# First layer's shift and scale biases as rows of a transposed parameter block, constants issued by ScalarE

## The reference, cut to what matters

```
ada = jax.nn.silu(cond) @ w_ada[l] + b_ada[l]            # w_ada[l]: 1024 x 6144, float32
sh1, sc1, g1, sh2, sc2, g2 = jnp.split(ada[:, None, :], 6, axis=-1)
u = layer_norm(x) * (1 + sc1) + sh1
m = even_mixer(u, w_in_even, ...)        # layer 0: attention and pooling; layer 1: conv and Fourier
x = layer_norm(ALPHA * x + g1 * (m @ w_out[l]), ln_g[l, 0], ln_b[l, 0])
u = layer_norm(x) * (1 + sc2) + sh2
x = layer_norm(ALPHA * x + g2 * conv_ffn(u), ln_g[l, 1], ln_b[l, 1])
```

## Time and profile before

| | before |
|---|---|
| median of 3 runs | 3036.16 us (3031.93 to 3036.25) |
| the profiled execution, its own time | 3033.15 us |
| its span | 3031.4 us |
| TensorE / VectorE / ScalarE / GpSimd busy | 91% / 52% / 31% / 14% |
| mean granted clock of TensorE | 0.959 |

### The profile page before, as it was taken

One profiled execution on the slowest core, in us unless ns is written; L12 is line 12 of the kernel. 1 busy time (PEld: TensorE's weight loads), 2 busy tenths in 40 slices (PEclk: granted clock), 3 DMA queues, 4 the chain that ended last, 5 costly groups with the idle time before them and its releaser, 6 DMA issues.

```text
span 3031.4 us, 36504 instructions
## 1 busy us (share of the span) xinstructions
PE 2768.7 (91%) x13992; PEld 2439.5 (80%) x13992; DVE 1565.9 (52%) x2166; ACT 936.5 (31%) x1417; POOL 419.2 (14%) x222
## 2 busy tenths in 40 slices
PE   5698799779999999999997899989899999999997
PEld 2387577558899999999994789968899999999996
DVE  0326688746555555555557333336555555555557
ACT  1611477635322222222225421124522222222123
POOL 0032377525000000000007000004200000000002
PEclk9799799979999999999998899989999999999999
DMA  8710100022311111111118231222311111111111
GB/s 291 258 46 6 42 1 1 7 78 77 132 42 42 42 42 42 42 42 42 38 37 288 67 91 42 69 77 77 125 42 42 42 42 42 42 42 42 42 35 77
DMA packets 172260, 202.26 MB, mean 67 GB/s; under 512 B 6843, under 2 KB 125207, under 8 KB 172179
## 3 DMA queue, kind: packets, MB, share of 16 engines
q1 hardware_dynamic: 171859, 200.83, 20.2%
q10 hardware_dynamic: 320, 0.33, 0.0%
HBM read 181.80 MB, written 19.33 MB: 66 GB/s over the span
## 4 chain that ended last, share of the span: by engine, by line
PE 69%; DVE 13%; ACT 6%; issue 5%; DMA 4%; POOL 2%; SPq 0%; ACTq 0%; DVEq 0%; POOLq 0%
PE ps L1845 37%; PE ps L2057 17%; PE ps L1823 7%; POOL p_low L749 2%; DMA late_w<-in_w_ada 2%; DVE small L1434 2%; DMA ada_w<-in_w_ada 2%; DVE dw_ctx L1269 1%; ACT ln_u L887 1%; DVE ft L1515 1%; PE ps L1977 1%; PE ps L1792 1%; DVE dctx L1537 1%; DVE uw L1269 1%; ACT p_top L812 1%
## 5 line engine op out<-in xcount | busy, mean ns | idle before, releaser
L1845 PE MATMUL ps<-act_b,uw 128*128 128x384 f32 x4608 | 819.5, 339 | 10.1 <-DVE act_b L1269 6.4
L1845 PEld LDWEIGHTS ps<-act_b,uw 128*128 128x128 f32 x4608 | 816.0, 189 | 11.9 <-DVE act_b L1269 6.9
L1845 PE MATMUL ps<-act_a,uw 128*128 128x384 f32 x3456 | 616.5, 340 | 5.5 <-DVE act_a L1269 5.5
L1845 PEld LDWEIGHTS ps<-act_a,uw 128*128 128x128 f32 x3456 | 613.1, 189 | 7.8 <-DVE act_a L1269 6.1
L2057 PE MATMUL ps<-dw,hh 128*128 128x512 f32 x2112 | 501.3, 397 | 8.7 <-DVE acc L1553 8.5
L2057 PEld LDWEIGHTS ps<-dw,hh 128*128 128x128 f32 x2112 | 398.6, 189 | 111.8 <-DVE acc L1553 10.3
L1553 DVE TENSOR_TENSOR acc<-acc,ps 128x512 f32<-128x512 f32 x360 | 246.6, 688 | 231.7 <-PE ps L2057 231.6
L812 ACT ACTIVATE fa<-ps 128x384 f32<-128x384 f32 (+2 forms) x176 | 67.4, 411 | 841.0 <-PE ps L1845 841.0
L1514 DVE TENSOR_SCALAR ft<-fa,fgrp 128x1153 f32<-128x1153 f32 x44 | 38.8, 882 | 450.8 <-ACT fa L812 450.8
L1269 DVE TENSOR_TENSOR uw<-raw_u,uw 128x1024 fp32r<-128x1024 f32 x112 | 136.9, 1223 | 127.0 <-ACT uw L812 123.3
L749 POOL TENSOR_TENSOR p_low<-p_exp,p_top 128x1536 fp32r<-128x1536 f32 (+1 forms) x50 | 170.8, 3416 | 93.4 <-ACT p_top L812 93.4
(11 more groups left out here) (201 smaller groups left out, 3170.7 us busy)
## 6 DMA issues: line engine op xcount, KB each, us to landing
raw_u<-in_w_up SPq DMA_DIRECT2D x88, 512.0 KB, 4.5
ada_w<-in_w_ada SPq DMA_DIRECT2D x64, 512.0 KB, 6.5
raw_d<-in_w_down SPq DMA_DIRECT2D x44, 512.0 KB, 3.7
late_w<-in_w_ada SPq DMA_DIRECT2D x32, 512.0 KB, 6.0
raw_u<-in_w_in_odd SPq DMA_DIRECT2D x20, 512.0 KB, 3.6
ln_y<-in_x_all SPq DMA_DIRECT2D x18, 512.0 KB, 5.2
xs<-ln_y SPq DMA_DIRECT2D x18, 512.0 KB, 2.6
acc<-xs SPq DMA_DIRECT2D x6, 1536.0 KB, 11.8
```

The costliest lines, as they stand in the source:

```text
L1845: mm = pe.matmul(out, uw[:, u_slot, w, k, :], src[:, k, a, c * CH:(c + 1) * CH], start=(k, w, a) == (0, 0, 0), stop=(k, w, a) == (KD - 1, ...
```

## The change

Three edits. The bias b_ada[0, 0:2048] is loaded as 16 rows of 128 into `prow[16:32, 3, :]`, transposed with the rest and kept in `par`, which grows from 220 to 236 columns; VectorE adds it (and 1 for the scales) when it writes `cols`. The 16 one-row products of line 1770 are gone, as are `bias_row`'s two first loads and their semaphore. `con` and the seven loads of weights and scales are issued by ScalarE; SyncE issues only c, c_ctx and the bias rows before the ada units. TensorE's first wait is for eleven loads.

```diff
@@ block.sync
-            sp.dma_start(con[:], t["k_con"]).then_inc(s_con, 16)
             sp.dma_start(prow[0:8, 3, :], t["c"]...).then_inc(s_con, 16)
             sp.dma_start(prow[8:16, 3, :], t["c_ctx"]...).then_inc(s_con, 16)
-            for l in range(2):
-                sp.dma_start(prow[0:66, l, :], t["ffn_conv_w"]...)
-                sp.dma_start(prow[66:88, l, :], t["ffn_conv_b"]...)
-            sp.dma_start(prow[0:18, 2, :], t["conv_w"]...)
-            sp.dma_start(prow[18:24, 2, :], t["conv_b"]...)
-            sp.dma_start(prow[24:28, 2, :], t["pool_scale"]...)
+            sp.dma_start(prow[16:32, 3, :], t["b_ada"][0:1, 0:2 * D].rearrange("a (k p) -> (a k) p", p=P)).then_inc(s_con, 16)
...
-            for n in range(2):
-                sp.dma_start(bias_row[n][0:1, :], t["b_ada"][0:1, n * D:(n + 1) * D]).then_inc(b_top, 16)
@@ block.scalar
+            act.dma_start(con[:], host["k_con"]).then_inc(s_con, 16)
+            for l in range(2):
+                act.dma_start(prow[0:66, l, :], host["ffn_conv_w"]...)
+                act.dma_start(prow[66:88, l, :], host["ffn_conv_b"]...)
+            act.dma_start(prow[0:18, 2, :], host["conv_w"]...)
+            act.dma_start(prow[18:24, 2, :], host["conv_b"]...)
+            act.dma_start(prow[24:28, 2, :], host["pool_scale"]...)
             act.wait_ge(setup_t, 4)
-            copy(par[:], ps[:, 0, 0:220]).then_inc(setup_c, 1)
+            copy(par[:], ps[:, 0, 0:236]).then_inc(setup_c, 1)
@@ block.vector
                     v.wait_ge(brow_mm, n + 1)
+                    if n < 2:
+                        v.wait_ge(setup_c, 1)
+                        v.scalar_tensor_tensor(cols[:, 0, n, :, :], ps[:, 6 + n, 0:2 * KD].rearrange("p (k c) -> p k c", c=2), float(n),
+                                               par[:, 220 + KD * n:220 + KD * (n + 1)].unsqueeze(2).broadcast_to([P, KD, 2]),
+                                               ALU.add, ALU.add).then_inc(cols_done, 1)
+                        continue
@@ block.tensor
-            pe.wait_ge(s_con, 16 * 10)
-            for o, rows, i in ((0, 88, 0), (88, 88, 1), (176, 28, 2), (204, 16, 3)):
+            pe.wait_ge(s_con, 16 * 11)
+            for o, rows, i in ((0, 88, 0), (88, 88, 1), (176, 28, 2), (204, 32, 3)):
...
-                pe.wait_ge(b_top, 32)
                 pe.wait_ge(ada_bank, 3 + ADA_TOP)
                 for n in range(2):
                     for k in range(KD):
-                        out = ps[:, 6 + n, 2 * k:2 * k + 2]
-                        pe.matmul(out, ada_top[...], con[:, C_FOLD:C_FOLD + 2], start=True, stop=False)
-                        mm = pe.matmul(out, bias_row[n][0:1, k * P:(k + 1) * P], con[0:1, C_SELB:C_SELB + 1].broadcast_to([1, 2]), start=False, stop=True)
+                        mm = pe.matmul(ps[:, 6 + n, 2 * k:2 * k + 2], ada_top[...], con[:, C_FOLD:C_FOLD + 2], start=True, stop=True)
                     mm.then_inc(brow_mm, 1)
```

More of the change, by code:

```diff
@@ L178, in build @@
         cols = fixed("cols", [P, 2, 4, KD, 2])
-        par = fixed("par", [P, 220])
+        par = fixed("par", [P, 236])
         conds = fixed("conds", [P, 48])
@@ L270, in sem @@
             return sems[name]
-        s_con, c_zero, b_top = sem("s_con"), sem("c_zero"), sem("b_top")
+        s_con, c_zero = sem("s_con"), sem("c_zero")
         setup_t, setup_c = sem("setup_t"), sem("setup_c")
@@ L326, in build @@
         xs = t["xs"]
+        host = t
         w_conv = t["w_in_odd"][0].rearrange("(k p) n -> p k n", p=P)
@@ L812, in copy @@
                 return act.activation(o, i, ACT.Copy)
+            act.dma_start(con[:], host["k_con"]).then_inc(s_con, 16)
+            for l in range(2):
+                act.dma_start(prow[0:66, l, :], host["ffn_conv_w"][l].rearrange("j (k p) -> (j k) p", p=P)).then_inc(s_con, 16)
+                act.dma_start(prow[66:88, l, :], host["ffn_conv_b"][l:l + 1].rearrange("a (k p) -> (a k) p", p=P)).then_inc(s_con, 16)
+            act.dma_start(prow[0:18, 2, :], host["conv_w"][0].rearrange("j (k p) -> (j k) p", p=P)).then_inc(s_con, 16)
+            act.dma_start(prow[18:24, 2, :], host["conv_b"].rearrange("a (k p) -> (a k) p", p=P)).then_inc(s_con, 16)
+            act.dma_start(prow[24:28, 2, :], host["pool_scale"].rearrange("a (k p) -> (a k) p", p=P)).then_inc(s_con, 16)
             act.wait_ge(setup_t, 4)
-            copy(par[:], ps[:, 0, 0:220]).then_inc(setup_c, 1)
+            copy(par[:], ps[:, 0, 0:236]).then_inc(setup_c, 1)
             act.wait_ge(c_zero, 1)
@@ L1767, in top_cols @@
                     for k in range(KD):
-                        out = ps[:, 6 + n, 2 * k:2 * k + 2]
-                        pe.matmul(out, ada_top[:, 2 * n + k // 4, (k % 4) * P:(k % 4 + 1) * P], con[:, C_FOLD:C_FOLD + 2], start=True, stop=False)
-                        mm = pe.matmul(out, bias_row[n][0:1, k * P:(k + 1) * P], con[0:1, C_SELB:C_SELB + 1].broadcast_to([1, 2]), start=False, stop=True)
+                        mm = pe.matmul(ps[:, 6 + n, 2 * k:2 * k + 2], ada_top[:, 2 * n + k // 4, (k % 4) * P:(k % 4 + 1) * P],
+                                       con[:, C_FOLD:C_FOLD + 2], start=True, stop=True)
                     mm.then_inc(brow_mm, 1)
```

## The result

The changed kernel takes 3013.73 us (median of 4 runs, 3011.05 to 3017.80), against 3035.46 us before (median of 4, 3031.93 to 3036.25). The ratio is 0.9932, 95% interval 0.9917 to 0.9947. The profiled execution took 3011.05 us, its span is 3009.2, where those of before were 3033.15 and 3031.4.

What follows compares the result with a forecast made beforehand. The prediction took the kernel to be bound by TensorE's products (busy 91%). Gains of 8.3 us (bias products) and 0.9 (earlier load stream) make 9.2, taken from the four executions' mean of 3034.4: 3025.2 us, range 3019 to 3032.

Steps and rivals of the forecast that it cites:

- 236 columns instead of 220 in a copy ... below 0.1 us: At the start: the wider copy into par, with 32 rows instead of 16 in the fourth transpose, costs below 0.1 us.
- from there on all stages of equal length: Expected sign: after the first projections' long run, near 140.3 us (149.46 before), every stage lasts as long as before.
- the higher clock: Upper bound for top_cols: remaining products run like line 1780's at the higher clock, saving 12.8 us instead of 8.3.
- 32 x 0.259 = 8.3 us: In top_cols, 35.63 to 52.20 us: removing 32 of 64 equally long records, 0.259 us each, saves 8.3 us.
- The stream is 0.9 us ahead: Ada loads for blocks 0 to 3: of 3.2 us earlier issue, 0.9 carries through, so top_cols starts 0.9 us earlier.
- VectorE's add at nothing: Writing cols: the add takes 0.2 us, between 0.17 and 0.69, which adds nothing that can be seen.
- Block 4 at 43.3: Block 4, started at 52.48 us before, starts at 43.3 after gains of 8.3 + 0.9 = 9.2 us.
- just ahead, so TensorE does not meet the bandwidth instead: At block 4's start: the units issued so far have landed by 42.4 us, ahead of block 4 at 43.3.
- a sign of being wrong: Listed signs: transposes after 12 us, ada stream still running at block 4's start, or the 9 us lost before the projections.
- The second one: Rival, chance 0.12: constants' completions seen only after the six ada units, first product 4.5 us late, gain 3.8: 3030.6.
- The first rival: Chance 0.12: ScalarE issues at SyncE's rate without the table load first, whole 3.2 us lead carries, 11.5 gained: 3022.9.
- the starving queue: Rival, chance 0.04: ScalarE's eight issues land late, first product 14.4 us late, net 6.1 us slower: 3040.5.

Runs made afterwards that it cites:

- e1: The kernel before with only par widened from 220 to 236 columns, which nobody reads: 3024.10 us against 3036.23, ratio 0.9958.
- e2: The changed kernel with par back at 220 columns and the bias columns in a buffer of their own, so old addresses: 3026.07 us, ratio 0.9970.
- e3: The kernel before without the 16 bias products, bias as rows, VectorE's add; constants still issued by SyncE, no buffer moved: 3025.03 us, ratio 0.9969.
- e4: The kernel before with only con and the seven loads of weights and scales issued by ScalarE: 3036.28 us against 3036.23, ratio 1.0001.
- e10: The changed kernel with one wait: SyncE issues ada loads only after all eleven constants have landed: 3011.41 us (2 runs), ratio 0.9919.
- e11: The kernel before with the 16 bias products writing columns of their own instead of accumulating, their number and shapes kept: 3033.61 us, ratio 0.9993.

## Why the prediction was wrong, point by point

- **"236 columns instead of 220 in a copy ... below 0.1 us": this is the step that failed.** I priced the copy and not the place of the buffers behind it. The 16 columns move `uw` against `act_a` and `act_b` by 64 bytes, and that is worth 12 us (e1). For the same reason "from there on all stages of equal length" was wrong. The prediction had named only one way in which the time could leave its range downwards, the higher clock, and that was not it. Without the move the kernel takes 3026.07 (e2), within 1 us of the forecast of 3025.2, but that nearness is luck. Up to block 4 the forecast was 9.2 us and e2's timeline shows 7.3: the products gave 1.3 more than forecast and the start 3.1 less. The other 3 us of e2's 10.2 lie within its interval, and no row accounts for them.
- **"32 x 0.259 = 8.3 us": right mechanism, size too small.** Measured 16.57 - 7.0 = 9.6 us (e3 against before). The remaining records do not keep their old spacing of 0.259 us but come every 0.219. The halving rested on the records of both kinds being equally long in the earlier trace rows; a record's length is not its share of the time when records overlap and alternate.
- **"The stream is 0.9 us ahead": wrong sign.** It was 1.8 us behind (e4 and the others). I took 0.5 us for the mixing of constants with ada loads; from the last issue to the transposes it was 4.95 us instead of 1.35, 3.6 us more. The transposes began at 8.70, not 7.5, and the first product at 11.56, not 10.3; then the free slots were used up and the stream nearly stood still from 12 to 15 us. ScalarE's issue rate, on the other hand, was better than assumed (0.43 us apart), and the table load came after the issues, not before.
- **VectorE's add at nothing: right.** 0.17 us, as the row that it replaced.
- **Block 4 at 43.3**: 45.12 in the changed kernel, 43.14 in e3. The step "just ahead, so TensorE does not meet the bandwidth instead" held only in its second half: the stream still moved 182 GB/s from 45 to 46 us, which the prediction had named as a sign of being wrong. It cost nothing, as block 4's first 24 records ran without a wait for a load. The lower end of the range, 3018.4, was written as 3019; 3013.73 lies below both.
- **The rivals.** The second one (constants behind the six units, `conds` at 15.0) named the right place but not the mechanism: `conds` was ready at 11.5, the constants landed at 8.70, and the units beside them moved bytes until past 11 us (346 GB/s from 11 to 12). The first rival and the starving queue did not occur. The Trainium skill's completion rule, quoted in the prediction ("DMA: Bandwidth & Descriptors", "Queues, rings and completion order"), would make the counts late: 4.9 us beside the ada loads (after), 1.4 without them (e10), agree in direction. But the data themselves were late, with the last packet at 8.06 us, and no row here shows counts held back behind the data of other loads. The Trainium skill's rule on the same page that several issuing engines save only sequencer time ("Issuing engines are not separate DMA queues") agrees as the upper bound it is: 3.2 us of issue time were saved, and nothing came of it.

The account for the whole: +9.6 products, -2.2 late constants in these two profiles, +15.4 up projections, -1.8 down projections (the 20 runs of 108 take 25.46 us where most took 25.36) makes 21.0 of the 22.2 us by which the spans differ. The remaining 1.2 us are not accounted for.

## What to carry to other kernels

A buffer that grows moves all that follow. Before the time of such an edit is put down to what it does, run it with the old addresses, or run the move alone; here the move was worth at least as much as the edit (12.1 against 10.2 us by the medians, 13.6 against 7.4 by the rows), and one unused buffer of the right size as much as both together (3009.51). A start that loads small constants and large weights at once should let the constants land first: here what waits for them was worth more than 3 us of the stream (block 4 at 43.11 in e10, 45.12 without the wait). And compare the durations of untouched loops in both profiles first of all: 0.57 us in 38 is easy to overlook and counts 22 times.

## What the runs showed of the hardware that was not expected

Streams of weight loads and products with 4-byte operands ran at a pace that depends on the distance in SBUF between the stationary and the moving operand, with a period that 256 bytes fits and 128 does not. At a granted clock of 1.00, 216 products of 384 columns took 38.0, 38.2, 37.5 and 37.5 us at distances of 128, 160, 192 and 0 modulo 256. 108 products of 512 columns took 25.4, 25.6, 25.5 and 24.8 us in the same kernels; there the moving operand is the one that was moved, so counted from the moving to the stationary operand, as for the first four, the distances are 128, 96, 64 and 0. Moving both together by 64 bytes changed nothing, and neither did other engines being busy or idle. That the two reads get in each other's way in SBUF is my reading of this; the runs show the distance, not the mechanism. Other distances were not tried.

Products of two columns whose contraction alternates between 128 rows and 1 row came every 259 ns at the lower clock; those of 128 rows alone every 219. Whether they accumulated on each other made no difference (16.57 us both ways, e11).
